# First attention of a two-block layer: a pair of heads becomes the same head of both key groups, scores run on 64-row halves, and VectorE takes one copy per pair in query tiles 1 to 3

## What is computed

```python
s_c = jnp.einsum('bqghd,bngd->bghqn', qg, k_cmp)
p_c = masked_softmax(s_c, cmp_end[None, :] <= tq[:, None])
imp = jnp.einsum('bghqn,nj->bgqj', p_c, overlap)       # summed over the heads of group g
score = jnp.where(valid_b, imp + FORCE_BONUS * forced, NEG_INF)
_, idx = lax.top_k(score, n_sel)                        # 8 blocks of 64 keys, per group
...
o = gc[..., 0:1] * o_c + gc[..., 1:2] * o_s + gc[..., 2:3] * o_w
```

## Time and profile before

| | |
|---|---|
| median of 3 runs | 2973.07 us (2971.09 to 2973.86) |
| profiled execution, own time | 2975.5 us |
| its span | 2973.7 us |
| PE busy | 2909.8 us (98%) |
| DVE, ACT, POOL busy | 1984.1, 1441.8, 467.7 us |
| mean granted TensorE clock | 0.99 |
| attention of the first block | from about 472 to 963 us of the span |

### The profile page before, as it was taken

The page is one execution under the profiler, slowest core; times in us unless marked ns, Lnnn a source line. Parts: engine busy times, 40 slices in busy tenths (PEclk is TensorE's granted clock), DMA queues, the critical chain, the costliest instruction groups (busy, mean ns, idle before and its releaser), DMA issues.

```text
span 2973.7 us, 42637 instructions
## 1 busy us (share of the span) xinstructions
PE 2909.8 (98%) x16332; PEld 2413.5 (81%) x16332; DVE 1984.1 (67%) x3262; ACT 1441.8 (48%) x2411; POOL 467.7 (16%) x764
## 2 busy tenths in 40 slices
PE   9999999889999999999999999999999999999998
PEld 6888888778988887888878888777877788888887
DVE  6653246766775349999989852475654877778864
ACT  4552125887776126555444431375643544444432
POOL 0110004765554120000000010261012000000000
PEclk9999997999999999999999999999999999999999
DMA  4222231000000511333344332000101244464232
GB/s 150 73 84 71 85 114 43 2 1 2 2 2 7 207 43 64 114 114 114 114 160 157 116 111 92 28 2 36 43 30 72 104 165 168 157 241 156 99 114 71
DMA packets 85383, 262.14 MB, mean 88 GB/s; under 512 B 10448, under 2 KB 13648, under 8 KB 84800
## 3 DMA queue, kind: packets, MB, share of 16 engines
q1 hardware_dynamic: 74208, 219.29, 20.3%
q0 software_dynamic: 10976, 40.15, 3.8%
HBM read 187.58 MB, written 66.06 MB: 85 GB/s over the span
## 4 chain that ended last, share of the span: by engine, by line
PE 89%; DVE 4%; ACT 4%; issue 2%; POOL 0%; DMA 0%; SPq 0%; ACTq 0%; DVEq 0%; POOLq 0%
PE PS L256 33%; PE PS L3136 23%; PE PS L3158 12%; PE PS L919 3%; PE PS L933 3%; PE PS L905 2%; PE PS L904 2%; PE PS L280 1%; PE PS L1563 1%; PE PS L1598 1%; PE PS L1585 1%; ACT P_SHORT L1003 1%; PE PS L956 1%; PE PS L3187 1%; ACT PT L1013 1%
## 5 line engine op out<-in xcount | busy, mean ns | idle before, releaser
L223 ACT CAST WHI<-RAW 128x1024 fp32r<-128x1024 f32 x100 | 104.8, 1049 | 589.4 <-PE PS L256 569.6
L228 DVE TENSOR_TENSOR WLO<-RAW,WHI 128x1024 fp32r<-128x1024 f32 x102 | 125.5, 1231 | 361.4 <-ACT WHI L223 360.1
L256 PE MATMUL PS<-HLO,WHI 128*128 128x512 f32 x992 | 306.2, 390 | 0.0
L3136 PE MATMUL PS<-XSH_T,PWH 128*128 128x512 f32 x596 | 233.1, 391 | 5.4 <-DVE PWL L2396 2.4
L3136 PE MATMUL PS<-XSH_T,PWL 128*128 128x512 f32 x596 | 231.9, 389 | 0.0
L3136 PE MATMUL PS<-XSL_T,PWH 128*128 128x512 f32 x596 | 231.9, 389 | 0.0
L3158 PE MATMUL PS<-DXH,PWH 128*128 128x512 f32 x560 | 218.1, 389 | 1.4 <-DVE DXL L2620 1.3
L256 PEld LDWEIGHTS PS<-HLO,WHI 128*128 128x128 f32 x992 | 186.5, 188 | 39.2
L3158 PE MATMUL PS<-DXL,PWH 128*128 128x512 f32 x560 | 217.9, 389 | 0.0
L3158 PE MATMUL PS<-DXH,PWL 128*128 128x512 f32 x560 | 217.9, 389 | 0.0
L3136 PE MATMUL PS<-XSH_B,PWL 128*128 128x512 f32 x456 | 177.4, 389 | 0.0
(11 more groups left out here) (443 smaller groups left out, 7225.6 us busy)
## 6 DMA issues: line engine op xcount, KB each, us to landing
W<-in_w SPq DMA_DIRECT2D x57, 1024.0 KB, 6.4
RAW<-in_w SPq DMA_DIRECT2D x104, 512.0 KB, 3.3
hidden<-W SPq DMA_DIRECT2D x54, 512.0 KB, 2.8
DXR<-hidden_t SPq DMA_DIRECT2D x20, 1024.0 KB, 5.1
DXR<-hidden SPq DMA_DIRECT2D x15, 1024.0 KB, 5.1
hidden_t<-W SPq DMA_DIRECT2D x24, 512.0 KB, 3.3
hidden_t<-T SPq DMA_DIRECT2D x16, 512.0 KB, 3.1
PLAIN_RAW<-hidden SPq DMA_DIRECT2D x14, 512.0 KB, 4.2
```

The costliest lines, as they stand in the source:

```text
L223: nc.scalar.copy(WHI[:, slot, :], RAW[:, slot, :]).then_inc(w_hi, 1)
L228: nc.vector.tensor_tensor(WLO[:, slot, :], RAW[:, slot, :], WHI[:, slot, :].bitcast(F32), ALU.subtract).then_inc(w_lo, 1)
L256: last = nc.tensor.matmul(o[:, half], w[:, slot, cols], x(k)[:, half], start=(k == 0 and w is WHI and x is hi), stop=(done and k == kcs - ...
L3136: last = nc.tensor.matmul(c.banks[q % 2][b], wt[n % 4][:, cols], xt[x][:, k, :], start=(opens and k == 0 and xt is c.xsh and wt is c.pwh), ...
```

## The change

A query tile now has no segments. A pair is head j of group 0 and head j of group 1, and:

- **Scores.** Queries and keys stand once, high and low part in tiles of their own (`QHI`, `QLO`, `KHI`, `KLO`), group 0 on rows 0 to 63 and group 1 on rows 64 to 127. A step is two matmuls of 64 rows, one for each group, in different PSUM banks; three steps (hi*hi, hi*lo, lo*hi) give the scores of both heads. `pe_scores` is called once for each branch, and in long tiles both branches of a group use the same banks: a branch's scores wait for both shifts of the branch before. Pieces of a long branch are split near the middle instead of at column 512.
- **Compressed branch.** Once for each query tile with both groups in one instruction (1024 elements where there were 512), 7 times in the loop instead of 15, and 16 matmuls of 64 rows for 8 of 128. `dve_cmp_first` does both groups. `PCG` goes away, the gate multiplies in place after the selection. In the loop the stages stand at places 0 to 5 of a tile's 8 pairs; sum, product and selection are all in place 3.
- **VectorE copies** the second chunk (`i == 1`) in tiles 1 to 3, behind the two shifts of the first branch.
- **Outputs, queries and keys** are taken by one instruction of 128 rows where there were two of 64.

```diff
+    def pe_scores(pe, m, branch):
+        qt, j = qt_of(m), m % HPG
+        pe.wait_ge(q_lo, qt + 1)
+        if not short(m):
+            pe.wait_ge(shifted, 4 * m + 2 * branch)
+        elif m:
+            pe.wait_ge(shifted, 4 * (m - 1) + 2 * branch + 2)
+        for c, end in parts_of(m, branch):
+            keys = slice(lo + c, lo + end)
+            for q, k in ((q_hi_t, KHI), (q_hi_t, KLO), (q_lo_t, KHI)):
+                for g in range(N_GROUPS):
+                    rows = half_of(g)
+                    last = nc.tensor.matmul(scores_of(m, branch, g)[:, c:end], q[rows, j, :], k[rows, branch, keys],
...
+    def dve_copies(m, batch, i):
+        return i == 1 if m < PAIRS_SHORT else batch[0] > 0 and (i - batch[0]) % 2 == 0
...
     def dve_attention(dve):
...
         for m in range(PAIRS_ALL):
             if ahead:
-                dve_shift(dve, 2 * ahead, 0)
-                dve_shift(dve, 2 * ahead, 1)
+                dve_shift(dve, ahead, 0, 0)
+                dve_shift(dve, ahead, 0, 1)
+            if short(m) and len(b[0]) > 1 and not waits_for_all(m):
+                dve_copy(dve, m, 1)
...
-            if m in SELECTED:
-                dve_select(dve, SELECTED[m])
+            if next_tile(m, 3):
+                dve_cmp_sum(dve, next_tile(m, 3))
...
+            if next_tile(m, 1):
+                dve_cmp_min(dve, next_tile(m, 1))
+            if next_tile(m, 3):
+                dve_select(dve, next_tile(m, 3))
...
     def pool_attention(pool):
...
             if ahead:
-                pool_probs(pool, 2 * ahead)
-                pool_probs(pool, 2 * ahead + 1)
+                pool_probs(pool, ahead, 0)
+            if next_tile(m, 3):
+                pool_cmp_probs(pool, next_tile(m, 3))
+            if ahead:
+                pool_probs(pool, ahead, 1)
...
+    def dve_select(dve, qt):
+        if qt:
+            dve.wait_ge(c_probs, qt)
+        seq(dve, nc.vector.tensor_reduce(IMPC[:, :, :], EC[:, :, :, :].rearrange("p g h n -> p g n h"), AX.X, ALU.add))
```

More of the change, by code:

```diff
@@ L638, in build, with act_keys_hi @@
+    QLO = [sb(f"QLO{i}", [HPG, P], X_AT + 8 * KB * i + 4 * KB, F32R) for i in range(2)]
+    N_KEYS = 2
     half_of = lambda g: slice(HEAD * g, HEAD * g + HEAD)
-    def act_keys_hi(act, g, other):
+    def act_keys_hi(act, branch):
         act.wait_ge(rope_done, len(ROPE))
         act.wait_ge(hid_mm, 2)
[L644 to L649, removed]
@@ L651, in act_queries_hi @@
-    def act_queries_hi(act, s):
-        rows, qt = half_of(s % 2), s // 2
-        act.wait_ge(rope_done, len(ROPE))
[L655 to L663, removed]
+        nc.scalar.copy(KHI[:, branch, :], KF[:, branch, :]).then_inc(k_hi, 1)
@@ L797, in batches_of, with next_tile @@
         return [range(0, first)] + ([range(first, n)] if first < n else [])
[L799 to L809, removed]
-    MASKED = {m + 1: s for m, s in SELECTED.items()}
-    N_SHORT = 4 * 2 * HPG
-    PAIRS_SHORT = N_SHORT // 2
-    TURN_BANKS = (T_PS[0], T_PS[1], C0_PS)
+    def dve_copies(m, batch, i):
+        return i == 1 if m < PAIRS_SHORT else batch[0] > 0 and (i - batch[0]) % 2 == 0
+    def next_tile(m, place):
+        return m // HPG + 1 if m % HPG == place and m // HPG + 1 < QT else None
+    TURN_BANKS = (T_PS[0], T_PS[1], C_FIRST[1])
     turned_at, used_at, c_turned_at, c_scored_at = [], [], [], [None]
@@ L938, in pe_cmp_values @@
     def pe_cmp_values(pe, m):
-        s, pair = m // PAIRS, m % PAIRS
-        wait_copied(pe, c_turned_at[s])
+        qt, j = qt_of(m), m % HPG
+        for g in range(N_GROUPS):
+            wait_copied(pe, c_turned_at[qt][g])
         if m > PAIRS_SHORT:
@@ L968, in pe_attention, with pe_cmp_turn @@
+    def pe_cmp_turn(pe, qt):
+        pe.wait_ge(c_gated, qt + 1)
+        for g in range(N_GROUPS):
+            c = c_turned_at[qt][g]
+            wait_turn_bank(pe, c)
+            for x in range(4):
+                last = nc.tensor.transpose(turn_ps(c)[:, P * x:P * x + P], EC[:, g, 2 * x:2 * x + 2, :], IDENT[:, :])
+            last.then_inc(t_done, 1)
     def pe_attention(pe):
-        pe.wait_ge(k_hi, 4)
-        pe.wait_ge(k_lo, 4)
+        pe.wait_ge(k_hi, N_KEYS)
+        pe.wait_ge(k_lo, N_KEYS)
@@ new lines, in dve_cmp_first @@
+        seq(dve, last)
+        for g in range(N_GROUPS):
+            last = nc.vector.tensor_tensor(MSEL[g][:, 0:P], MSEL[g][:, 0:P], TRI[:, :], ALU.add)
+        seq(dve, last)
+    def dve_out_lo(dve, m):
+        dve.wait_ge(o_hi, m + 1)
+        nc.vector.tensor_tensor(out_of(HLO, m), out_ps(m), out_of(O_HI, m).bitcast(F32), ALU.subtract)\
+            .then_inc(o_free, 1)
+    def dve_attention(dve):
+        for m in range(2):
+            for branch in range(2):
+                dve_shift(dve, m, branch, 0)
+                dve_shift(dve, m, branch, 1)
+                if m or branch:
+                    dve_inverse(dve, m if branch else m - 1, 1 - branch)
+        dve_inverse(dve, 1, 1)
```

486 lines of the change are left out of this document (238 added, 248 removed).

## The result

The changed kernel took 2996.04 us (median of 4 runs, 2995.15 to 2997.35), the kernel before 2973.47 us beside it (4 runs, 2971.09 to 2975.84). The ratio is 1.0074, with a 95% interval of 1.0058 to 1.009: slower by 0.6 to 0.9%. The prediction was 2995.0.

What follows compares the result with a forecast made beforehand. PE bounds the long tiles, ACT's list also counts in tiles 1 and 2, and DVE's at the start. Terms -11 - 3 - 5 + 2 + 5.7 + 27 + 6 = +22 us on 2973.07 gave 2995 us, range 2981 to 3012.

Steps and rivals of the forecast that it cites:

- Scores in halves: PE's scores in tiles 4 to 6: both row halves run at once, less added changes of form; -11 us.
- Tile 7: Last tile: its 0.53 us gain for a pair is taken as lost, because PE waits for ACT's copy.
- Compressed scores: PE's compressed scores: both groups in halves cost one group's 1.73 us, saving 0.45 a tile; -3 us (bounds 0 and -10).
- ACT: ACT's list: one output cast less for a pair, one copy less in tiles 1 to 3; -5 us (bounds 0 and -10).
- the copy on DVE: Tile 3: DVE's copy behind two shifts ends after PE's fourth chunk could start; +2 us, with changes of form.
- Start: Before the first tile: DVE's first selection chain handles twice the elements ahead of L388, so PE starts later; +5.7 us.
- The selection at place 3: Place 3, tiles 0 to 6: DVE's late selection delays the next pair's shifts, so PE waits; +27 us (bounds 10 and 38).
- The walk for tile 5: Tile 5 timeline from PE's first scores: product ends at 10.2 us, selection at 14.1, and PE stands 4.1 us.
- The clock: Behind six PE waits of 4 to 6 us the clock falls to half, 1 us each; +6 us (bounds 0 and +30).
- The first rival: The selection is in time: PE stands nowhere behind it and the clock holds; 2962 us, chance 0.17.
- The third rival: The halves do not overlap in fp32r, so scores cost twice 95 us; +95, about 3085 us, chance 0.04.
- The fourth rival: The clock stays low behind each wait, as after the start: +30 instead of +6, 3019 us, chance 0.07.

Runs made afterwards that it cites:

- experiment 7: Changed kernel with group 1's scores taken from group 0's query and key rows, so both groups run on the same row half: 3092.57 us (two runs).
- experiment 12: Kernel of experiment 9 with the turn of the compressed probabilities on PE and its copy on ACT moved from place 6 to 7: 2954.81 us.
- experiment 3: Changed kernel with the copy of the second chunk in tiles 1 to 3 back on ACT instead of DVE: 2986.14 us.
- experiment 1: Changed kernel with POOL's compressed product in place 3 moved ahead of its two probability products for the pair ahead: 2977.95 us.
- experiments 6: Kernel of experiment 5 with the selection in halves, group 0 ending place 3, group 1 place 4; gate, turn, copy one place later, L662 moved: 2970.68 us.
- 9: Kernel of experiments 6 with each selection half cut again, all but the head sum behind the next pair's first shifts; masks, gate, L662 moved: 2988.5 us.
- experiment 5: Changed kernel with the changes of experiment 1 and experiment 3 together: 2972.92 us.
- experiment 4: Changed kernel with PE's score matmuls reordered: three steps of one half, then three of the other, instead of alternating: 2995.12 us.

## Why the prediction was right

The direction, the size and the main mechanism held: the late selection, and PE waiting behind it. That the sum came within 1 us of the measured time was partly luck, because errors of both signs met.

- **Scores in halves, predicted -11.** They overlap (experiment 7), at 0.17 and 0.12 us for a step. Plain pairs went from 7.85, 8.31 and 8.99 us to 7.35, 7.95 and 8.57: 0.50, 0.36 and 0.42 less, where 0.46, 0.42 and 0.48 were taken; for 8 pairs each that is -10.2. (For tile 5 the prediction's worked sum gives 0.76 and its list 0.72, which makes 0.3 us over 8 pairs.)
- **Tile 7, predicted 0.** It won 3.9 us. Its plain pairs lost 0.25 (10.17 to 9.92), the largest single part is in the pair that had compressed work of the second segment (11.85 us before, 9.92 after). That pair's gain belongs mostly to the compressed scores. The wait for ACT's copy that was to eat the gain grew less than was taken: to 0.54 us in a pair, from 0.31 to 0.45.
- **Compressed scores, predicted -3.** In tile 5 the pairs with compressed work cost 4.9 us above plain ones before (10.50 + 10.50 + 8.59 + 8.54 less 4 x 8.31); in experiment 12, where nothing is waited for, 3.8 (9.07 + 10.59 less 2 x 7.95): 1.1 us a tile in place of 0.45.
- **ACT, predicted -5, and the copy on DVE, +2.** Tiles 0 to 3 of experiment 12, which has no such copy, take 181.9 us against 189.1: 7 less. The size is near -5, but it does not bear the term out: it came without the copy that the term counted on, tile 1, where ACT is the fullest, has only 0.5 us of it (tiles 0, 2 and 3 have 2.1, 2.5 and 2.1), and the compressed scores are in it too. What ACT's shorter list gave was not measured by itself. (PE's waits for ACT's copies before were the 11.7 us at L919 that the prediction names, and 3.7 more at L933.) The price of the copy was right away from the selection: tile 3's plain pairs went from 6.43 to 6.58 us, and to 6.31 without it (experiment 3).
- **Start, predicted +5.7** (its terms add up to 5.6). L388 began at 476.54 in place of 471.22, 5.3 later; PE waited 6.7 us there, not 8. The first compressed values came 7.4 us later: the way there from PE's first scores took 11.8 us in place of 9.7. The clock was at 0.50 there in both kernels, so it does not explain these 2.1 us; the turns and the compressed scores of both groups now stand in that stretch.
- **The selection at place 3, predicted +27.** The waits are 31.7 us. In tiles 4 to 6 they were to be 3.9, 4.1 and 4.3 and are 3.2, 3.9 and 3.7; in tiles 1 to 3 17 and are 17.6; in tile 0 2.5 and 3.2. One reason in the walk was wrong: that scores two pairs ahead would hide most of the wait in tiles 1 to 3 if the copy were not there. Experiment 3 has no such copy, and 10.3 us are still waited there. The 5 us taken off for waits that were there anyway were too much. The walk for tile 5 placed the end of the product at 10.2 us after the first scores and the selection's end at 14.1; from 782.3 on, when the scores began, they came at 10.2 and 13.9.
- **The clock, predicted +6.** This term was mis-sized: 1 us for each of six waits was taken, and experiment 1 shows 2.1 on average in tiles 4 to 6. If all six cost as much, it is 13; in tiles 1 to 3 it was not measured. The estimate took 3 us at half clock, from one short stretch. In windows of 1 us the clock was 0.50 from 725 to 733 in tile 4 and from 797 to 804 in tile 5, some 7 us each, and PE was busy in all of what lay behind the wait. Over the whole attention it stood at 0.50 for 89 us, where it had been 34; 41 and 31 of these belong to the start.

Experiment 12, in which hardly anything behind the start is waited for, parts the sum in two. It is 20 us below the kernel before, where the sum without waits, clock and copy has 13 (-11 - 3 - 5 + 5.7); and the waits, the clock and the copy cost the 41 us between it and the changed kernel, where the sum has 35 (27 + 6 + 2). So the gains were some 7 us larger than taken and the losses some 6, and the sum shows only the difference. The terms one by one do not add up so closely, because they overlap.

The first rival, the selection in time at 2962 us, is a kernel that can be built, but not by the order in POOL's list alone. Experiment 1 met the condition that I gave for the product and still waited 2.25 us. The condition on the shift, at most 0.6 us late, needed the selection cut up (experiments 6 and 9), and then its followers moved (12): 2954.8. The third rival was excluded by experiment 7; its price for the score steps was right by the pair (1.8, 1.9 and 2.1 us in tiles 4 to 6), and that the whole came so near to its 95 us is partly chance, since the clock is in it. (Its time should be 2995 + 95 = 3090 by its own sum, not 3085.) The fourth rival's clock did not stay low: behind each wait in the loop of the changed kernel it was back at 1.00 within some 10 us, and it stayed at 0.50 for longer only behind the start.

What stays open: what holds the clock at 0.50 behind the start, for 31 us in the kernel before and for 38 to 75 in the others, behind waits of 1.6 as of 6.8 us for L388. PE's idle time does not tell it: from 489.8 to 503 in the changed kernel PE was busy in all 13.2 us and the clock stood at 0.50 throughout, while from 517 to 547 it was busy in 24.5 of 30 us at full clock. Nor does the wait's length tell in the loop, as experiment 5 showed.

## What to carry to other kernels

When two stages are merged into one of twice the size, an engine that was never the bound can become it for a few microseconds: look for each long instruction group that stands in one piece ahead of something PE needs every few microseconds, and measure the room there (here 1.0 to 1.6 us in a pair of 8 us) before choosing its place. Cut it to pieces that fit, then walk all that hangs on it, on every engine, and move each by as much; stopping halfway cost 18 us here and finishing gave 34 back. A wait of PE is to be priced with the slow clock behind it: here 3 to 4 us of wait were some 6 of time.

## What the runs showed of the hardware

**Two matmuls on the two row halves did not have to be neighbours in the list.** In experiment 4 the list had three steps of one half and then three of the other, and the time (2995.12 against 2996.04) and the records were those of the alternating list. The Trainium skill (TensorEngine Tiling (Array Packing), Key Properties) states that tiles operate independently, which these numbers bear out for three instructions in a row.

**VectorE and GpSimd held each other up.** The same instruction L662 (128x1024, both inputs in SBUF) took 1.20 us at its fastest and 2.97 at its slowest:

```profile
L662 DVE TENSOR_TENSOR QLO<-Q,QHI x8: 1204/1534/2972, 461.9 to 874.6; 128x1024 fp32r<-128x1024 f32 x8
```

The slow one began at 589.37, 0.01 us behind GpSimd's product, which ran its usual 1.90 us to 591.26, and ended 1.08 after it. In tile 0 VectorE was first, by 0.04 us, and the product took 2.92 us:

```profile
504.16 2.92 POOL L1146 TENSOR_TENSOR EC<-EC,CINV 128x1024 f32<-128x1024 f32 x1
```

```profile
504.12 1.20 DVE L662 TENSOR_TENSOR QLO<-Q,QHI 128x1024 fp32r<-128x1024 f32 x1
```

In the four meetings of the attention (tiles 0 to 3) the one that started first ran at its own speed, and the other took longer by nearly the first one's time. The Trainium skill (SBUF — State Buffer, Who interferes with whom) says the same of the port pair that the two engines share; the trace agrees, with 1.0 and 1.8 us of delay. In the changed kernel this pair of instructions meets in each of tiles 0 to 3, right ahead of the selection. The prediction's walk did not have it. By these starts it put the selection off by about 1.0 us in tile 2 (592.27, with the product done at 591.26) and as much in tile 0 (the product at 2.92 in place of 1.90); that is an estimate. Experiment 6 and those built on it, in which L662 has left place 3 of the short tiles, change other things along with it, so its share of the waits was not measured by itself.
